# Mixture-of-experts stores: one per expert for the wide rows and one for the narrow rows, in place of two and four

## The reference, cut to what matters

```python
def hier_moe(h, w_group, w_sub, w_gate, w_up, w_down):
    ...                                     # a token picks 2 of 16 experts and their gates
    hid = jax.nn.silu(jnp.einsum('btd,edf->btef', h, w_gate)) * jnp.einsum('btd,edf->btef', h, w_up)
    hid = hid * gates.astype(h.dtype)[..., None]
    return jnp.einsum('btef,efd->btd', hid, w_down)
```

## Time and profile before

| | us |
|---|---|
| median of three runs | 1474.75 |
| lowest, highest | 1472.49, 1483.41 |
| the profiled execution's own time | 1480.49 |
| its span, first to last instruction | 1478.7 |
| first store of an expert's result, layer 0 / layer 1 | 507.1 / 1293.2 |
| first gather from `slots_y`, layer 0 / layer 1 | 659.71 / 1443.93 |

### The profile page before, as it was taken

One profiled execution on the slowest core, in us unless ns is written; L12 is line 12 of the kernel. 1 busy time (PEld: TensorE's weight loads), 2 busy tenths in 40 slices (PEclk: granted clock), 3 DMA queues, 4 the chain that ended last, 5 costly groups with the idle time before them and its releaser, 6 DMA issues. The chain is left out here.

```text
span 1478.7 us, 29953 instructions
## 1 busy us (share of the span) xinstructions
PE 1305.8 (88%) x11855; PEld 770.3 (52%) x11855; DVE 723.8 (49%) x1881; ACT 411.2 (28%) x1098; POOL 176.3 (12%) x247
## 2 busy tenths in 40 slices
PE   6999999998799998976999989868778699899897
PEld 3445565565356654534555545445454355755543
DVE  4435777676655311137343544377874465411123
ACT  3024445453210211133213121134455211121112
POOL 2002223322011000013021100100100001000002
PEclk9999999999898899997999999988988799799998
DMA  6150435223804899994465899799999631899935
GB/s 231 58 149 6 134 107 182 74 77 131 288 36 170 308 367 356 320 329 169 150 220 218 329 347 361 302 405 374 408 378 343 219 140 52 339 379 343 338 94 189
DMA packets 133902, 348.15 MB, mean 235 GB/s; under 512 B 22603, under 2 KB 52478, under 8 KB 125566
## 3 DMA queue, kind: packets, MB, share of 16 engines
q1 hardware_dynamic: 115378, 311.53, 59.0%
q10 hardware_dynamic: 13388, 16.82, 3.4%
q0 software_dynamic: 4992, 17.83, 3.3%
HBM read 302.61 MB, written 43.52 MB: 234 GB/s over the span
## 5 line engine op out<-in xcount | busy, mean ns | idle before, releaser
L409 PE MATMUL bank<-wring,xT 128*128 128x512 f32 x448 | 200.4, 602 | 0.0
L409 PEld LDWEIGHTS bank<-wring,xT 128*128 128x128 f32 x448 | 84.1, 192 | 100.6 <-issue 100.5
L1440 PE MATMUL bank<-wring,xT 128*128 128x512 f32 x256 | 120.2, 623 | 2.0 <-DVE xT L1360 2.0
L883 PE MATMUL bank<-xT,wring 128*128 128x512 f32 x256 | 113.7, 602 | 3.9 <-DVE hgrn_g L707 3.9
L2803 DVE STREAM_TRANSPOSE attn_k_pages<-attn_k_pages 128x1024 f32<-128x1024 f32 x64 | 77.6, 1232 | 40.4 <-DMA attn_k_pages<-cache_k 39.9
L883 PEld LDWEIGHTS bank<-xT,wring 128*128 128x128 f32 x256 | 48.7, 192 | 65.3 <-issue 59.8
L1440 PEld LDWEIGHTS bank<-wring,xT 128*128 128x128 f32 x256 | 49.6, 200 | 60.1 <-issue 59.9
L2803 DVE STREAM_TRANSPOSE wring<-wring 128x1024 f32<-128x1024 f32 x44 | 52.5, 1222 | 49.2 <-DMA wring<-cache_k 49.2
L785 DVE COPY_PREDICATED gla_att<-level_masks,bank 128x512 f32<-128x512 int32 x48 | 35.1, 731 | 72.1 <-PE bank L903 72.0
L2316 PE MATMUL bank<-xT,wring 128*128 128x512 f32 x128 | 56.9, 597 | 0.0
L903 PE MATMUL bank<-gla_qe,gla_ke 128*128 128x128 f32 x384 | 49.9, 285 | 0.0
(11 more groups left out here) (460 smaller groups left out, 2403.2 us busy)
## 6 DMA issues: line engine op xcount, KB each, us to landing
attn_k_pages<-cache_k SPq DMA_DIRECT2D x64, 512.0 KB, 7.6
wring<-cache_v SPq DMA_DIRECT2D x56, 512.0 KB, 7.8
wring<-cache_k SPq DMA_DIRECT2D x44, 512.0 KB, 7.0
moe_wd<-moe_w_down SPq DMA_DIRECT2D x20, 1024.0 KB, 13.6
attn_shared<-cache_v SPq DMA_DIRECT2D x40, 512.0 KB, 5.7
wring<-moe_w_gate SPq DMA_DIRECT2D x18, 1024.0 KB, 11.2
wring<-moe_w_up SPq DMA_DIRECT2D x18, 1024.0 KB, 14.8
wring<-a_w_in SPq DMA_DIRECT2D x16, 1024.0 KB, 10.5
```

The source lines that it names most:

```text
L409: last = nc.tensor.matmul(bank[:, :], xT[:, c, cols(t)], w[:, c, :], start=(c == 0), stop=(c == DC - 1))
L883: last = nc.tensor.matmul(bank[:, :], lhsT, k.xT[:, c, 0:SEQ], start=(c == 0), stop=(c == DC - 1))
L1440: last = nc.tensor.matmul(bank[:, :], k.xT[:, c, cols(t)], w[:, c, :], start=(c == 0), stop=(c == DC - 1))
```

## The change

The two wide stores become one, and the four narrow ones become one. The source is the whole tile of 128 partitions. The target is the block of rows in `slots_y`, viewed as (column part, row, column), so that the partitions of a column part fall on its columns. `STORES` falls from 6 to 2 with the number of transfers, and with it all waits on `y_out`.

```diff
-NB, STORES = 2, 6
+NB, STORES = 2, 2
...
         eng.wait_ge(self.y_v, j + 1)
-        for n in range(4):
-            eng.dma_start(self.slot_rows(row, WIDE, NARROW)[:, n * 2 * P:(n + 1) * 2 * P], self.YN[u][n * NARROW:(n + 1) * NARROW, :])\
-                .then_inc(self.y_out[u], 16)
+        eng.dma_start(self.slot_rows(row, WIDE, NARROW).rearrange("r (n c) -> n r c", n=4), self.YN[u][:, :])\
+            .then_inc(self.y_out[u], 16)
...
-            for n in range(2):
-                act.dma_start(self.slot_rows(row, 0, WIDE)[:, n * HB:(n + 1) * HB], self.YW[u][n * WIDE:(n + 1) * WIDE, :])\
-                    .then_inc(y_out[u], 16)
+            act.dma_start(self.slot_rows(row, 0, WIDE).rearrange("r (n c) -> n r c", n=2), self.YW[u][:, :])\
+                .then_inc(y_out[u], 16)
```

## The result

The changed kernel takes **1592.9 us** (median of 4 runs, 1588.6 to 1597.5) against 1479.1 (4 runs, 1472.5 to 1484.2) for the kernel before beside it: 1.0771 times as long, with an interval of [1.0733, 1.0809]. The forecast was 1613, in a range of 1560 to 1680, and slower with a chance of 0.90. Sign and mechanism came out; the cost is 114 us where 138 were forecast.

What follows compares the result with a forecast made beforehand. The two to four DMA engines carrying the merged stores were taken to pace PE: 79 + 55 + 8 - 4 = +138 us, giving a median of 1613 us, in a range of 1560 to 1680.

Steps and rivals of the forecast that it cites:

- Which engines a store runs on: Expert stores: the target's first count sets the engines, 2 for the wide store and 4 for the narrow one.
- The alternative that the rows of before left open: Expert stores: pieces spread over as many engines as there are pieces, up to 16; time 1474 us, chance 0.10.
- The rate: Loaded DMA engines in the expert stages: 24.8 GB/s for loads, 23.2 for stores; lower bound 21.8.
- Layer 0: Layer 0's expert stage: the most loaded engines' work makes it 231.5 us, +79.
- Layer 1: Layer 1's expert stage until the last load: the loaded engines' work makes it 164.7 us, +55.
- Layer 1's end: After layer 1's last experts: the last two experts' stores delay the gather from 1443.93 to near 1452.1, +8 us.
- POOL's gathers: Layer 0's first two gathers: seemingly held by a DVE instruction, which would be through before the later stores; -4 us.
- Where it waits: PE in the expert stages: waits name loads and, in down, ACT's or DVE's copies; rounds stretch to 15 or 17 us.
- ACT and SP issue fewer transfers, nothing: Store issue on ACT's and SP's queues: shorter issue time gains nothing, since PE waits for loads and stores.
- rival 2: Output buffers: two aren't enough, copies wait for stores; 96 us extra, 1709 us, if loads run dry each round; chance 0.08.
- The clock: PE's granted clock in layer 0: more waits may lower it; nothing in the sum, allowed for in the range.

Runs made afterwards that it cites:

- linear: Changed kernel with both merged stores' target taken as 128 rows one behind the other (outputs not the reference's): 1477.9 us against 1476.8 for the kernel before, ratio 1.0002.
- 62 rows: Kernel before with each of its two wide stores split by rows into 62 and 2: 1568.1 us, ratio 1.062.
- 60 rows: Kernel before with each of its two wide stores split by rows into 60 and 4: 1476.6 us against 1475.9, ratio 1.0006.
- narrow alone: Kernel before with the four narrow stores made one and the two wide ones kept: 1480.7 us, ratio 1.002.
- wide alone: Kernel before with the two wide stores made one and the four narrow ones kept: 1561.8 us, ratio 1.058.
- SP issues: Changed kernel with both stores of each layer's first ten experts issued by SP instead of ACT: 1593.8 us against 1477.7 for the kernel before, ratio 1.0785.
- dve_early: Kernel before with one of DVE's two 4.42 us products at layer 0's end made earlier, while experts still run: ratios 0.9974 and, repeated, 0.9963.

## Why the prediction was right, and where it was off

**Which engines a store runs on: right for this change.** There are 10,628 packets, and the order of the pattern alone, all in which linear and the change differ, is worth all of the time. The alternative that the rows of before left open, as many engines as pieces up to 16, is refuted by 62 rows on two. So is the forecast's own wording taken as a general rule: the first count itself, up to 16, would give 62 rows 16 engines. For 2 and 4 the count and its largest divisor are the same number, so the sum didn't feel it.

**The rate: the term that was mis-sized.** Layer 0 was given +79 and cost +69.2. Its work on a loaded engine is 2.938 + 16 x 0.1638 = 5.559 MB, and 5.559 / 221.8 us is 25.1 GB/s. I had 24.8 for loads, from a stretch of the attention stage, and 23.2 for stores, 6% less from the shares of the earlier trace rows; in the totals no such discount shows. With 25.1 for all, layer 0 is +69, which is no check, as 25.1 is taken from it. Layer 1 is one: it is 3.959 / 25.1 = 157.7 us until the last load, +48, and with the tail +55, where 52.3 was measured and 63 forecast. The sum would have been 69 + 55 - 4 = +120, for a measured +117.0 of the span. The same quotient, MB on the most loaded engine by the stage's time, for each kernel in layer 0:

| kernel | MB | us | GB/s | ratio to before |
|---|---|---|---|---|
| before | 3.33 | 152.6 | 21.8 | |
| linear | 3.33 | 150.3 | 22.2 | 1.0002 |
| 60 rows | 3.40 | 154.2 | 22.0 | 1.0006 |
| narrow alone | 3.73 | 156.2 | 23.8 | 1.002 |
| 62 rows | 5.17 | 207.6 | 24.9 | 1.062 |
| wide alone | 5.17 | 206.9 | 25.0 | 1.058 |
| SP issues | 5.56 | 221.0 | 25.2 | 1.0785 |
| after | 5.56 | 221.8 | 25.1 | 1.0771 |

A loaded engine does 25 GB/s, but 16 together do 21.8 each (349 in the earlier trace rows). Up to 25 / 21.8, some 15% more on one engine by this estimate, the common limit covers it; of imbalances that small only one was run, 12%. That is the part of the argument that the forecast hadn't drawn: its lower bound for the rate was the common limit, its upper bound came within 2% of what the four kernels with 55% or more on top show.

**Layer 1's end: +8 forecast.** From PE's last product of the experts to the first gather it is 13.6 us where it was 4.5, so +9.1. In layer 0, where I also wrote 10 us longer, it is 20.3 for 4.6, +15.7, over half as much again as forecast; that lies inside its sum.

**POOL's gathers: -4 forecast, -4.4 measured**, and dve_early bears the cause out.

**Where it waits: wrong.** I wrote that PE's waits would name loads and, in down, ACT's or DVE's copies. PE has no wait for a token load left in layer 0; it waits for the silu, behind ACT held in an issue. The forecast's line "ACT and SP issue fewer transfers, nothing" failed in detail: the narrow store's issue takes 8.4 us at the median and 17.5 at most, in place of 2.02. sp_issues shows that it made no odds to the time. Rounds are 221.8 / 16 = 13.9 us on average, not 15 to 17 (9.5 before, by the same count), and uneven: from one expert's first transposed product to the next it is 9.5 to 23.1 us. The landing times that I named can't be read, as the view gives hardly any for these issues. One can be bounded: ACT's last copy of the stage, at 716.81, waited 12.0 us for expert 13's stores, whose issue began at 690.72. They took about 26 us to land, and the two buffers made ACT's and DVE's copies wait, 35.1 and 31.5 us in all, as rival 2 had feared.

**Rival 2, no extra: right.** Had the loaded engines run dry each round, the quotient would have fallen below 25, and fewer than two packets would be under way for more than 0.6% of the stage. The quotient is the same for kernels with two stores held on ACT, on SP, and with five or eight smaller ones.

**The clock.** Layer 0's granted clock fell from 0.98 to 0.84, between the two levels of 2.4 and 1.2 GHz, and PE's busy time there rose from 138.6 to 149.5 us. No term was given to it. The stage is the loaded engines' work with 25.1 GB/s at this clock, so I take the added 11 us of PE to lie in its waiting; no run separates them.

## What to carry to other kernels

Before merging transfers, look at the outermost count that the pattern is left with: on the queues of ACT and SP the largest divisor up to 16 of it is the number of DMA engines, and 62 rows are as bad here as 2. Count a queue's packets less its data pieces to read that number from a profile, and take the time of a stage as the bytes on its most loaded engine, which costs next to nothing (0.2%, not told from none) at 12% over the mean and 5.8% at 55% over; by the rates above the turn lies near 15%, which is an estimate. A mean DMA share that falls while a queue is held in issuing is the sign of it; moving the issue from ACT to SP moved the wait and not the time.

## What the chip showed that I had not expected

- The issue of one narrow store held ACT for up to 17.5 us and, in sp_issues, SP for up to 10.5, while the wide store just ahead of it took 0.55 at the median (6.0 at most).
- A loaded DMA engine reaches 25.1 GB/s, stores in 1 and 2 KB pieces among its work, against 21.8 when all are busy.
- Fewer transfers gained nothing: six stores or two, at 16 engines each, 1.0002 [0.9974, 1.003].
- Through POOL's queue the change's patterns cost 1.6% and not 7.7%.
- Beside a 4.42 us product on DVE an indirect gather of POOL's took 4.01 us, and 0.87 without. Moving one of the two products gave 0.9974 [0.9946, 1.0002] and 0.9963 [0.9937, 0.9989], the one version here that seems faster than both kernels, by about 0.3%.
